# The front of an encoder layer: modulation rows in four groups of 32 columns, an eleven piece ring, and unread products between the sums of squares

## The reference, cut to what matters

```python
mod = silu(c) @ w_ada + b_ada                     # c: one row of 1024 for each of the two groups
sh1, sc1, g1, sh2, sc2, g2 = split(mod, 6)
h = modulate(rmsnorm(x, norm1_g), sh1, sc1)       # y * (1 + sc1) + sh1
proj = h @ w_in                                   # q, k, v | hyena x1, x2, v | two gates
attn = windowed_gqa_sink(rope(q), rope(k), v, sink)
spec = rfft(taps(sin-MLP filter, w3, decay))      # hyena_filter_spectra, needs only tables and weights
hy = hyena_branch(proj, conv, spec, bias)
merged = sigmoid(gate_a) * (attn @ w_attn_o) + sigmoid(gate_h) * (hy @ w_hyena_o)
x = x + g1 * (merged @ w_out)
h = modulate(rmsnorm(x, norm2_g), sh2, sc2)
x = x + g2 * (square(relu(h @ w_up)) @ w_down)
y = modulate(rmsnorm(x, final_g), shf, scf)
```

## Time and profile before

| | |
|---|---|
| median of three runs | 1204.16 us (1203.9, 1204.16, 1209.77) |
| the profiled execution's own time | 1207.46 us |
| its span, first to last instruction | 1205.7 us |
| mean granted TensorE clock | 0.988 |
| PE busy, share of the span | 97% |
| DVE, ACT | 57%, 30% |
| start of `gemm(2)`, the first product after the front | 75.20 us |

### The profile page before, as it was taken

The page is one execution under the profiler, slowest core; times in us unless marked ns, Lnnn a source line. Parts: engine busy times, 40 slices in busy tenths (PEclk is TensorE's granted clock), DMA queues, the critical chain, the costliest instruction groups (busy, mean ns, idle before and its releaser), DMA issues.

```text
span 1205.7 us, 17346 instructions
## 1 busy us (share of the span) xinstructions
PE 1170.6 (97%) x6580; PEld 1074.1 (89%) x6580; DVE 691.9 (57%) x1146; ACT 363.5 (30%) x550; POOL 73.4 (6%) x104
## 2 busy tenths in 40 slices
PE   6989999999999999999999999999999999999997
PEld 1576669888899999999989999999999999999886
DVE  3877788887755555566546677553465432333434
ACT  3541114544531211141325431123211331122314
POOL 1100110000001211100000000000000000000000
PEclk8989999999999999999999999999999999999998
DMA  8833456222242332174322243331233212112212
GB/s 296 341 114 105 138 176 218 71 88 71 66 154 96 121 125 97 61 279 158 111 72 90 96 136 133 135 108 53 71 122 103 70 52 70 61 61 70 70 35 105
DMA packets 42529, 138.68 MB, mean 115 GB/s; under 512 B 4539, under 2 KB 10251, under 8 KB 41452
## 3 DMA queue, kind: packets, MB, share of 16 engines
q1 hardware_dynamic: 26832, 83.19, 20.1%
q0 software_dynamic: 10592, 41.95, 9.7%
q10 hardware_dynamic: 5052, 12.81, 3.1%
HBM read 122.20 MB, written 15.74 MB: 114 GB/s over the span
## 4 chain that ended last, share of the span: by engine, by line
PE 90%; DVE 6%; issue 1%; DMA 1%; ACT 1%; SPq 0%; DVEq 0%; ACTq 0%
PE acc_ps L562 64%; PE acc_ps L634 11%; PE wk L857 3%; PE wk L681 2%; PE wk L835 2%; DMA mod_raw<-in_w_ada_rows 1%; PE wk L776 1%; PE wk L797 1%; PE acc_ps L641 1%; PE wk L786 1%; PE wk L674 1%; DVE dot_out L1408 1%; PE wk L595 1%; DVE w_lo L1315 1%; DVE filt_red L1459 0%
## 5 line engine op out<-in xcount | busy, mean ns | idle before, releaser
L562 PE MATMUL acc_ps<-act_hilo,w_hi 128*128 128x384 f32 x2304 | 506.5, 341 | 5.6 <-DVE act_hilo L1361 4.2
L562 PEld LDWEIGHTS acc_ps<-act_hilo,w_hi 128*128 128x128 f32 x2304 | 407.7, 189 | 26.1 <-issue 22.3
L562 PE MATMUL acc_ps<-act_hilo,w_lo 128*128 128x384 f32 x1152 | 293.7, 335 | 0.0
L1315 DVE TENSOR_TENSOR w_lo<-w_raw,w_hi 128x1024 fp32r<-128x1024 f32 x102 | 124.4, 1220 | 173.5 <-ACT w_hi L1009 172.5
L562 PEld LDWEIGHTS acc_ps<-act_hilo,w_lo 128*128 128x128 f32 x1152 | 209.3, 189 | 0.0
L1009 ACT ACTIVATE w_hi<-w_raw 128x1024 fp32r<-128x1024 f32 x102 | 107.7, 1056 | 286.8 <-PE acc_ps L562 283.2
L562 PE MATMUL acc_ps<-hidden_hilo,w_hi 128*128 128x384 f32 x768 | 164.0, 334 | 0.0
L562 PEld LDWEIGHTS acc_ps<-hidden_hilo,w_hi 128*128 128x128 f32 x768 | 135.9, 188 | 0.0
L562 PE MATMUL acc_ps<-hidden_hilo,w_lo 128*128 128x384 f32 x384 | 97.4, 334 | 0.0
L1720 DVE SCALAR_TENSOR_TENSOR xT<-acc_ps,modT,xT 128x384 f32 (+2 forms) x72 | 30.4, 478 | 89.9 <-PE acc_ps L562 89.3
L562 PEld LDWEIGHTS acc_ps<-hidden_hilo,w_lo 128*128 128x128 f32 x384 | 69.4, 188 | 0.0
(11 more groups left out here) (211 smaller groups left out, 1295.5 us busy)
## 6 DMA issues: line engine op xcount, KB each, us to landing
dot_ring<-in_w_ada_cols POOLq DMA_DIRECT2D x52, 512.0 KB, 3.7
w_raw<-in_w_pre SPq DMA_DIRECT2D x50, 512.0 KB, 3.4
w_raw<-in_w_up SPq DMA_DIRECT2D x32, 512.0 KB, 3.3
w_raw<-in_w_down SPq DMA_DIRECT2D x32, 512.0 KB, 3.3
mod_raw<-in_w_ada_rows SPq DMA_DIRECT2D x12, 512.0 KB, 8.7
spec<-filt_out POOLq DMA_DIRECT2D x12, 512.0 KB, 3.1
gate_spill<-gates_out ACTq DMA_DIRECT2D x16, 384.0 KB, 2.3
hy_spec<-spec SPq DMA_DIRECT2D x12, 512.0 KB, 5.4
```

Of the source, the lines that this page charges most:

```text
L562: mm = pe.matmul(acc_ps[:, slot, 512 * h:512 * h + HALF], w[:, kw, :], src[:, x, k, HALF * h:HALF * h + HALF], start=(first and i == 0), s ...
L1315: dve.tensor_tensor(lo, raw[s][:], hi, ALU.subtract).then_inc(lo_done, 1)
```

## The change

1. The shift and scale of all eight slices are made on PE: four groups of 512 columns (`MODS = 4`), each with two blocks of shift and two of scale. The four dot products of scale on DVE and their loads are gone. DVE's dot products elsewhere stay (48 in all, before 52).
2. The two columns of silu(c) are padded to 32 (`cpad`). Slice k's product goes to partitions 32 (k mod 4) on, so that four slices stand in four groups of 32 columns of the array and each adds up two slices. ACT copies all 128 partitions, and the turning product, with a selecting column pair (`V_SEL`), adds the four groups.
3. The ring has eleven pieces (five in `mod_raw`, six in `mod_raw_b`, which lies where the ring of the dot products and `c_rows` lie later). SP and POOL issue the pieces in turn.
4. x comes first, in eight single slices, the even ones on SP and the odd ones on POOL.
5. PE's order: all sums of squares and the norm come before the modulation rows; between the sums of squares stand seven products of 256 columns that nobody reads (`warm`), one for each of `n_acc` 2 to 7 and one behind `norm_sum`.
6. DVE's second filter layer (`arg_turns(1)`, `arg_rest(1)`, and its last step as `arg_clamp`) stands among the norm's steps, and `w3_pair` ahead of tile 0. On POOL the filter's weights and tables are issued right behind the pieces, and `c_rows` and the dot products' first loads wait for all 32 modulation products.

```diff
-DOTS = 52
-DOT0 = 12
-SDOT = 4
+DOTS = 48
+DOT0 = 16
-MODS = ((SH1, 0), (SC1, 0), (SH1, 4))
-MRING = 5
+MODS = 4
+MRING = (5, 6)
...
+        def mod_bank(g):
+            return wk[:, 1024 + 512 * (g % 2):1536 + 512 * (g % 2)]
...
+        def mod_load(q, p):
+            if p >= sum(MRING):
+                q.wait_ge(m_used, 2 * (p - sum(MRING)) + 2)
+            g, i = divmod(p, 4)
+            q.dma_start(mod_piece(p), w_adaP[g, :, 2 * i:2 * i + 2]).then_inc(ld_mod[p], 16)
...
             sp.dma_start(vT[:], a["vec"]).then_inc(ld_vec, 16)
-            mod_load(0)
-            mod_load(1)
-            sp.dma_start(xT0[:, 6:8], a["x_T"][:, 6:8]).then_inc(ld_x[3], 16)
...
+            for k in range(0, KD, 2):
+                x_load(sp, k)
+            mod_load(sp, 1)
             weights(0)
...
             weights(1)
...
+            for p in range(5, 4 * MODS, 2):
+                mod_load(sp, p)
...
+            for k in range(1, KD, 2):
+                x_load(pool, k)
+            for p in (0, 2, 3, *range(4, 4 * MODS, 2)):
+                mod_load(pool, p)
...
-                o = acc_ps[0:2, 1, 512:1024] if g == 1 else wk[0:2, 1024:1536]
-                pe.matmul(o, cact[:, k:k + KD + 1:KD], mraw[:, 2 * (p % MRING) + k % 2, :],
-                          start=(k == 0), stop=(k == KD - 1)).then_inc(m_used, 1)
+                pe.matmul(mod_bank(g)[32 * (k % 4):32 * (k % 4) + 32], cpad[:, k, :], mod_piece(p)[:, k % 2, :],
+                          start=(k < 4), stop=(k >= KD - 4)).then_inc(m_used, 1)
...
+            def warm(n):
+                for _ in range(n):
+                    pe.matmul(wk[:, 1024:1280], ident[:], ones[:].rearrange("p (o n) -> p o n", o=1).broadcast_to([P, 2, P]),
+                              start=True, stop=True)
...
+            for k in range(2, KD):
+                pe.wait_ge(n_acc, k)
+                warm(1)
+            norm_sum(0)
+            warm(1)
+            norm_spread(0)
...
             def filt_start():
-                act_e.wait_ge(dot_done, 2 * SDOT)
...
-            scale_in(0)
...
-                if t == 0:
-                    w3_pair()
-                    arg_turns(1)
                 if t == 1:
-                    arg_rest(1)
-                    rope(0)
                     dve.wait_ge(z_hi, 1)
...
                     w3_low()
+                    rope(0)
```

More of the change, by code:

```diff
@@ L500, in _ @@
                     dot_load(DOT_BESIDE[f] + 3)
-            for n in range(SDOT + 15, DOTS_OUT):
+            for n in range(15, DOTS_OUT):
                 dot_load(n)
@@ L699, in _ @@
             turn_c()
-            for k in range(6):
-                mod_row(0, k)
             pe.wait_ge(ld_filt, 16)
@@ L732, in _ @@
             first(1, 2)
+            for k in range(KD):
+                mod_row(3, k)
+            first(0, 4)
             first(1, 3)
-            for k in range(4, KD + 1):
-                if k < KD:
-                    first(0, k)
-                if k >= 5:
-                    first(1, k - 1)
+            mod_turn(3)
+            for k in range(5, KD):
+                first(0, k)
+                first(1, k - 1)
+            first(1, KD - 1)
             def rope_turn(j):
@@ L1115, in filt_start @@
                 act_e.activation(zst[:], zh[:], ACT.Copy).then_inc(z_hi, 1)
+                for i, src in enumerate((w3s[:], w3[:, 0:1024])):
+                    act_e.wait_ge(w3_sum, i + 1)
+                    act_e.activation(w3h[:, i], src, ACT.Copy).then_inc(w3_hi, 1)
             specs = []
@@ L1403, in scale_in, with dot @@
+            def dot(n):
+                mt = DOT0 + n
+                i = n % 3
+                dve.wait_ge(ld_dot[i], 16 * (n // 3 + 1))
                 if n == 0:
                     dve.wait_ge(ld_c, 16)
-                for g in range(2):
-                    if n + g:
-                        dve.wait_ge(dot_done, 2 * n + g)
-                    dve.tensor_tensor_reduce(junk[:], ring[:, n % 3], cb[:, g], 1.0, ba1[:, k:k + 1],
-                                             ALU.mult, ALU.add, sc1[:, k, g:g + 1]).then_inc(dot_done, 1)
@@ L1457, in arg_rest, with arg_clamp @@
                     dve.wait_ge(f_sin, 1)
-                for part, src in ((TWO_PI_A, fa), (TWO_PI_B, fb), (TWO_PI_C, fb)):
+                for part, src in ((TWO_PI_A, fa), (TWO_PI_B, fb)):
                     chain(dve.scalar_tensor_tensor(fb[h], fk[h], -part, src[h], ALU.mult, ALU.add))
+            def arg_clamp(layer):
+                h = slice(0, P if layer else 64)
+                chain(dve.scalar_tensor_tensor(fb[h], fk[h], -TWO_PI_C, fb[h], ALU.mult, ALU.add))
                 dve.tensor_scalar(fb[h], fb[h], 3.1415925, -3.1415925, ALU.min, ALU.max).then_inc(f_arg, 1)
-            for k in range(6):
+            for k in range(KD):
                 norm_acc(k)
             arg_first(0)
-            norm_acc(6)
-            norm_acc(7)
             arg_turns(0)
@@ L1655, in _ @@
             run = {"turn": turn_low, "forward": products, "inverse": combine}
+            w3_pair()
             for t in range(T_MERGE):
```

233 lines of the change are left out of this document (106 added, 127 removed).

## The result

| | before | after |
|---|---|---|
| median of the runs | 1204.36 us (1203.9 to 1209.77, four runs) | 1190.42 us (1186.96 to 1193.0, four runs) |
| ratio | 1 | 0.9872, 95% interval 0.9835 to 0.991 |
| the profiled execution | 1207.46 us | 1186.96 us |
| its span, mean granted clock | 1205.7 us, 0.988 | 1185.3 us, 0.997 |

The kernel became faster by 1.3% (14 us) in the medians and by 20.5 us between the two profiled executions. The profiled one of after was its fastest, that of before lay 3 us above its median. So 14 to 18 us is the gain, and the 20.5 us are what the two traces can be compared on.

What follows compares the result with a forecast made beforehand. PE held 90% of the chain, with the front delaying `gemm(2)`. Terms -13.6 + 0.2 - 4.0 = -17.4 us, against the median of 1204.16, gave 1186.8, predicted as 1187 us, range 1181 to 1200.

Steps and rivals of the forecast that it cites:

- Step 1: x's loads and sums of squares: last slice lands at 13.2 us, last add ends about 15.3 instead of 27.57.
- Step 2: PE before the norm: six unread products take 5.2 us at half clock, delaying it about 4; spread ends at 24.1.
- Step 3: Modulation products: four column groups at once, 1.9 us a group; first `norm_h` at 29.1 instead of 42.73, term -13.6 us.
- Step 4: First `norm_h` to `gemm(2)`: dot products removed, groups, turns and filter steps added; 32.6 us against 32.4, term +0.2.
- Step 5: Behind `gemm(2)`, to `filt_unit(0)`: less DVE work there; wait -2.6 us, clock -1.4, in all -4.0.
- Two at a time: Modulation products: only two column groups run at once, 3.6 us a group; +5.1, 1192 us; chance 0.15.
- one at a time: Modulation products run one after another, 6.9 us a group; +18.5, 1205 us, no change; chance 0.09.
- The turn slower: Modulation products one after another, PE at half clock through groups 0 and 1, 13.7 us each; 1219 us; chance 0.05.
- The clock rival: Front: clock falls in a new gap, about 4 us, or the norm runs cold, 3; 1190 to 1191 us; chance 0.13.
- the ring: Modulation pieces' buffers: the eleventh piece gates only pieces 11 to 15, waits ending at 25 to 30 us; no term.

Runs made afterwards that it cites:

- e12: Changed kernel with each queue's first modulation piece issued ahead of its slices of x: 1194.34 us, 0.9903 of the kernel before.
- e3: Changed kernel with all eight slices of a modulation group in one column group instead of four: 1212.23 us, 1.0049 of the kernel before.
- e4: Changed kernel with slices alternating between two column groups instead of four: 1198.51 us, 0.9933 of the kernel before.
- e5: Changed kernel with `w3_pair` and DVE's second filter layer put back behind the front, and ACT's order with them: 1195.1 us, 0.9904 of the kernel before.
- e1: Changed kernel run again unchanged, in the series of the other experiments: 1188.49 us against 1206.49 for the kernel before, ratio 0.986.
- e2: Changed kernel without the seven unread products: 1192.61 us, 0.9891 of the kernel before.
- e9: Changed kernel with six more unread products in PE's waits and modulation pieces held until each queue's third x slice landed: 1187.69 us, 0.984 of the kernel before.
- e10: Changed kernel with six more unread products in PE's waits and four ahead of the filter's first layer: 1189.82 us, 0.9854 of the kernel before.
- e7: Changed kernel with x's slices 2 and 5 issued by ACT, behind the filter's inputs: 1192.91 us, 0.9889 of the kernel before.

## Why the prediction was right

Forecast 1187 us in a range of 1181 to 1200; measured 1190.42, and 1188.49 in the second series. Between the profiled executions the sum forecast 17.4 us, and 20.5 were measured.

| step | forecast | measured |
|---|---|---|
| 1: last slice of x; last add ends | 13.2; 15.3 | 15.3; 18.2 |
| 2: norm's sum; spread ends | 20.0; 24.1 | 18.3; 22.3 |
| 3: group of 16 records; first `norm_h` | 1.9; 29.1 (-13.6) | 1.93; 27.04 (-15.7) |
| 4: `norm_h(0)` to `gemm(2)` | 32.6 (+0.2) | 31.9 (-0.6) |
| 5: `gemm(2)` to `filt_unit(0)`; its wait | 13.7; 0.6 | 14.0; 0.76 |
| 5: wait and clock | -2.6, -1.4 | -2.3, -1.6 |

**Step 1** was 2.1 us short at the landing and 2.9 at the last add. The bytes themselves came as counted. The queues of the changed kernel in its first 13.2 us (packets, MB, share of the 16 engines):

```profile
q0 software_dynamic: 367, 1.77, 38.5%
q1 hardware_dynamic: 678, 1.57, 37.6%
```

POOL's queue had moved more than its four slices (1.57 MB) by then, SP's nearly so, and still the last square waited until 15.3. Either packets of the pieces go in between or a landing is signalled some time behind its last bytes; no run tells them apart. e12 supports the counting of bytes ahead in a queue for differences (2.3 us where it said 2.6).

**Step 2** had the opposite error. It added the six unread products behind the filter's layer one after another at half clock, 5.2 us, and had them end at 20.0. They ended as the last add did: the layer began at 9.74, not at 12, and the twelve records took 5.98 us from 12.46 on, among them three waits for DVE's adds (1.4 us in all). What was called a delay of 4 us beyond the data is none. The two errors partly cancel, which is luck, and the front came 2.1 us earlier than forecast, most of the 3.1 us by which the sum was short.

**Step 3** was the bold one, four at a time where rows showed two, and it is confirmed by the series 7.05, 3.63, 1.92 us (e3, e4, changed). What a change to narrow products and back costs can be read at group 2. The plain records before it start 0.17 us apart, so their last slot ends at 36.02, and the group begins at 36.11. Its 16 records at 0.43 us and four at a time would be through at 37.82, and the next plain product begins at 37.97. That is 0.09 and 0.15 us, about 1 us for all eight changes, within the 1.2 that the prediction allowed. The Trainium skill's rule that a change of tiling mode drains TensorE (TensorEngine Tiling (Array Packing), Tiling Modes) does not contradict this; if there is a drain here, it costs no more than that.

**Step 4**, the lay-out of the three orders side by side, held within 0.7 us over 32: turn 2 was to end at +14.2 and ended at +14.1, group 3 to start at +16.3 and did at +16.2, `first(0,5)` at +23.5 and did at +22.9.

**Step 5** is shown by e5: the wait (3.04) and the dip of the clock (0.86) come back together when DVE's work is put back. One reading behind it was wrong. The prediction took the half clock behind `filt_unit(0)` to be the dip in the third slice of the earlier trace rows; that dip is the stretch from 61.5 to 68.4 us, ahead of `gemm(2)`, and the one behind `filt_unit(0)` is in the fourth slice. So no row that it names shows the 1.4 us of that term. That it came out near the 1.6 measured is luck in the source, though not in the mechanism.

**The rivals.** Two at a time was forecast at 1192 and one at a time at 1205; made on purpose they gave 1198.5 and 1212.2. Both lie 6 to 7 us higher, and 5 us higher when taken against e1 (10.0 for 5.1, 23.7 for 18.5). I had let PE's waits absorb more of the longer products than they did (the full pace is 6.8 and 20.5), and I had left the clock out of these two prices. The turn slower was priced at 13.7 us each for groups 0 and 1, at half clock throughout, with 1219. e3 shows it in part: its groups 0 and 1 took 7.7 and 8.8 us, each partly at half clock, and the whole came out slower than before (1.0049), mostly by the pace. The clock rival (a fall in a new gap, or a cold norm: 1190 to 1191) did not occur in the two traces of the changed kernel, but both halves of it occur in traces of variants, at lower prices: a fall costs 1.1 us at `gemm(2)` (e5, e12), not 4, and a cold norm 1.8 (e5), not 3. The median of 1190.42 is in that rival's range, so the medians do not tell the forecast from it; only the profiled pair does. What I called costless or left unpriced, the ring, was worth 12 us; the sum had it as a condition (group 3 in time) and so came out right, but a reader could not have told its price from it.

**Open.** The medians gained 14 and 18 us where the profiled pair gained 20.5. That other executions of the changed kernel lost the clock in the front, as e2's and e5's did, fits their range (1186.7 to 1193), but they have no trace. Their mean granted clocks are on record: 0.993, 0.990 and 0.993 in the three slower ones of the first series, against 0.997 in the profiled one, which would be 5 to 8 us and thus enough; but in e1 0.996 against 0.998, which would be 2.4 of the 4.4 us between its slowest and its fastest. So the clock is a large part of the scatter, and not shown to be all of it. Nor was it tried to put DVE's argument of layer 0 behind the norm's multiplication, the one edit that the chain of waits asks for now, since that argument holds both ways to `norm_h(0)`; e9 shows only that earlier data alone is not enough.

## What to carry to other kernels

When a product has few weight columns, spread the contraction over column groups: here its time fell in proportion to their number (7.05, 3.63, 1.92 us). Before an operation is sped up by earlier data, ask what else on the same engine stands between it and the end: e9 took the last wait for x away and gained nothing, since four adds on DVE stood behind the slices before it in any case. Unread products help where they reach up to the work that they are meant for; put earlier, with a gap behind them, they did not (e10). A ring that lets two queues run ahead can be worth more than the arithmetic it feeds. It shows in the DMA's GB/s per window, and its price may fall due far from the ring, at a table that now shares the DMA with late loads.

## What the runs showed of the hardware

- Four float32 products of 32 weight columns, in four column groups, run at once: 16 records of 512 columns in 1.92 us, against 3.63 in two groups and 7.05 in one.
- The granted clock fell to half while PE was busy, in products of one column group (36.1 us, e3), of two (30.0, e4), in the filter's second layer of a kernel with four (29.8, e2), and in plain products of full width behind a wait of 1.65 us (40.3, e4). In waits of about 1.4 us it fell in e5, e7 and e12, and in the same waits of the changed kernel it did not.
- The recorded granted clock stood at 1.00 in the first microseconds even where durations were those of the lower level (e2: 2.69 us for what takes 1.53).
- What stood ahead of x in a queue delayed it: 0.52 MB on each of two queues, last slice at 17.63 us instead of 15.32 (e12). Moving part of x to a third queue that had other loads made it land later (e7: squares still waited for a slice until 16.51 us).
- Holding the other loads back (e9) brought the last slices in at 14.5 us or sooner, where nine traces with the same order of x have 14.75 to 15.91, and left the DMA at 326 GB/s from 10 to 20 us instead of 394.
- A change from plain products to products in four column groups and back showed 0.09 and 0.15 us (group 2 of the changed kernel).
